# Root-mean-square norm: the last halving of the squares moves from VectorE to TensorE, and the last output tile is scaled on GpSimd

## The chip, the cores and the metric

The kernel runs on one core of a Trainium2 chip. The metric is the device time in microseconds of one execution; lower is better. One execution was profiled; the span of its profile runs from the first to the last instruction.

## The reference

Two layers (DEPTH = 2) work on x, 256 tokens by 1024 channels, in float32. Each begins with a root-mean-square norm, then a wide projection, three mixing branches (a recurrent one, a stick-breaking attention, a differential attention), gates, and an output projection that is added to x. A second norm feeds a convolutional feed-forward network, also added to x. A last norm gives the output. What matters here is the norm, five times in all:

```python
def rms_norm(x, g):
    xf = x.astype(jnp.float32)
    y = xf * lax.rsqrt(jnp.mean(xf * xf, axis=-1, keepdims=True) + EPS)
    return (y * g.astype(jnp.float32)).astype(x.dtype)

for l in range(DEPTH):
    h = rms_norm(x, norm_mix_g[l])          # norm 0 and norm 2
    ...
    x = x + merged @ w_out[l]
    x = x + conv_ffn(rms_norm(x, norm_ffn_g[l]), ...)   # norm 1 and norm 3
return rms_norm(x, norm_final_g)            # the last norm
```

## The kernel before

The activations lie transposed: 1024 channels are 8 tiles (KT) of 128 partitions, the 256 tokens (T) are the free dimension. The weights come as a stream of slabs of 128x1024 float32 through a ring of four buffers. SyncE issues the loads. ScalarE rounds a slab to a high half (`hi`), VectorE subtracts to get the low half (`lo`, line 1305), and TensorE multiplies with three products for each 128x128 block (`split_mm`: high by high, high by low, low by high). The activations are split in the same way into `hh` and `hl`. Each product is a matmul of 128x128 by 128x256.

Each engine has its own instruction list and runs it in order. For the mixing part the order is written out by hand: `STEPS` for TensorE, `ACT_STEPS` for ScalarE, `DVE_STEPS` for VectorE. A step `D n` is a slab (TensorE multiplies it; the other two split slab n+3), `E n` empties its result, and the steps of the branches lie between. The feed-forward part comes after these lists, as a loop over turns. Semaphores tie the lists together.

The norm is not applied to x before the product. The raw x, times the gain, is split and multiplied at once, and the factor of a token (`rs`) is applied when a result is emptied. So TensorE can start on slabs before the factor is known. To get the factor:

- ScalarE squares the 8 tiles of x into `XSQ`.
- VectorE adds them in halves in `add_squares`: 4 tiles on 4 (128x1024 elements), 2 on 2 (128x512), 1 on 1 (128x256, line 1321). `own.mark` and `own.wait` order one addition behind the other on VectorE; `DVE_OWN["layer"]` is the number of such marks in a layer. The last addition raises `squared`.
- TensorE in `norm(n)` multiplies an all-ones 128x128 block with the one tile that is left. This sums over the partitions and puts the sum of each token in every partition of bank 4, columns 0 to 255. For even n (the mixing part) two more matmuls, with the squares as the stationary operand and one column of ones as the moving one, put the sums as columns 256 and 257, token by partition: the value projections need the factor in this form. Odd n (the feed-forward part) doesn't use it.
- ScalarE in its own `norm(n, b, w)` takes a logarithm and an exponential of w columns (line 915 is the helper through which its activations go), and raises `rms_inv`. VectorE multiplies what it empties by `rs`.

TensorE runs norm 0 and norm 2 behind slab D2, norm 1 and norm 3 behind the first two slabs of the feed-forward part. Line 468 is the helper `mm`, so nearly all matmuls carry this line.

The last norm is written out at the end: ScalarE and VectorE scale the eight tiles of x by the gain into `HF`, TensorE sums squares, ScalarE makes `rs`, then VectorE multiplies four pairs of tiles of `HF` by `rs` (128x512 elements each, line 1801). SyncE stores each pair behind its `y_ready` (line 435), 256 KB each. GpSimd has little to do: clearing a block of constants once in a layer (line 450), and a few transfers; its last is the load of parameters that is issued when the last convolution is done.

Of the kernel before, what the change touches and what calls it, by code (L numbers as in the profile page):

```python
# [34 lines left out]
ALU = mybir.AluOpType  # L35
# [144 lines left out]


ACT_OWN = {"turn": 0, "layer": 16}
DVE_OWN = {"turn": 8, "layer": 125}


class Own:
# [16 lines left out]
def hybrid_blocks(nc, x_t, w_in, mix_in, ffn_in, fin_in, cf_in, cb_in, y_out):  # L203
    DEPTH = w_in.shape[0] // SLABS
    with ExitStack() as ctx:
# [144 lines left out]
        partner_in = [sem("query_partners_in"), sem("key_partners_in")]  # L350
        gates_ready = sem("gates_ready")
        merged_b, merged = sem("merged_b"), sem("merged")
        y_ready, y_stored = sem("y_ready"), sem("y_stored")
        last_scaled, square_pairs = sem("last_scaled"), sem("square_pairs")
        up_scaled, low_out = sem("up_scaled"), sem("low_out")
        rated_x, rated_h, rated_l = sem("rated_x"), sem("rated_h"), sem("rated_l")
# [57 lines left out]
        @block.sync  # L414
        def _(sp):

            sp.dma_start(raw[:, 0, HALF[0]], w_in[0, :, HALF[0]]).then_inc(first_in, 16)
            sp.dma_start(pm[:, 0:UPS], mix_in[0, :, 0:UPS]).then_inc(mix_in_s, 16)
            sp.dma_start(raw[:, 0, HALF[1]], w_in[0, :, HALF[1]]).then_inc(raw_in[0], 16)
            sp.dma_start(x[:, X_PART[2], :], x_t[:, X_PART[2], :]).then_inc(x_in[2], 16)  # L420
            for s in (1, 2):
                sp.dma_start(raw[:, s], w_in[s]).then_inc(raw_in[s], 16)
            sp.dma_start(cf[:, :], cf_in).then_inc(const_in, 16)
            sp.dma_start(raw[:, 3], w_in[3]).then_inc(raw_in[3], 16)
            sp.dma_start(cb[:, :], cb_in).then_inc(const_in, 16)
            sp.dma_start(pm[:, UPS:], mix_in[0, :, UPS:]).then_inc(ups_in_s, 16)
            with sp.Fori(1, DEPTH * SLABS // RING + 1) as i:
                for s in range(RING):

                    sp.wait_ge(hi_done, RING * i + (s - RING + 1))  # L430
                    sp.wait_ge(lo_done, RING * i + (s - RING + 1))
                    sp.dma_start(raw[:, s], w_in[RING * i + s]).then_inc(raw_in[s], 16)
            for b in range(4):
                sp.wait_ge(y_ready, b + 1)
                sp.dma_start(y_out[:, 2 * b:2 * b + 2, :], HF[:, 2 * b:2 * b + 2, :]).then_inc(y_stored, 16)
            sp.wait_ge(y_stored, 64)
            sp.wait_ge(ups_in_s, 16 * DEPTH + 16)
            sp.wait_ge(mix_in_s, 16 * DEPTH + 16)
            sp.wait_ge(ffn_in_s, 16 * DEPTH + 16)
            for s in range(RING):  # L440
                sp.wait_ge(raw_in[s], 16 * (DEPTH * SLABS // RING + 1))

        @block.gpsimd
        def _(pool):
# [3 lines left out]
            for l in range(DEPTH):  # L448
                pool.wait_ge(act_["kk"], n_of("kk", l, 1))
                pool.memset(BX, 0.0).then_inc(ones_set, 1)  # L450
                pool.wait_ge(ones_set, 3 * l + 1)
                for a in range(2):
                    pool.memset(BX[:, BASE * a:BASE * a + 33 * (BASE - 1) + 1:33], 1.0).then_inc(ones_set, 1)
                pool.wait_ge(act_["o"], n_of("o", l, BT))
                for i in range(2):
                    pool.wait_ge(*n_out(l, (OUT_CQ, OUT_CK)[i]))
                    for m in range(2):
                        for b in range(2):
                            to, of = HD * m + 8 * b, HD * m + 8 * (1 - b)
                            pool.dma_start(PARTNER[i][to:to + 8], (qc, kc)[i][of:of + 8, :, :])\  # L460
                                .then_inc(partner_in[i], 16)
                pool.wait_ge(conv_done, l * 2 * FT + 2 * FT)
                pool.dma_start(pf[:, :], ffn_in[l + 1]).then_inc(ffn_in_s, 16)

        @block.tensor
        def _(pe):
# [100 lines left out]

            def norm(n):

                pe.wait_ge(squared, n + 1)  # L570
                last = mm(bank[4][:, 0:T], cst("ones"), XSQ[:, 0, :], True, n % 2 == 1)
                if n % 2 == 0:

                    for tok in range(2):
                        last = mm(bank[4][:, T + tok:T + tok + 1], XSQ[:, 0, tok * P:(tok + 1) * P],
                                  cst("ones")[:, 0:1], False, True)
                last.then_inc(pe_["norm"], 1)

            def step(l, s):
# [326 lines left out]
        def _(act):  # L906
# [307 lines left out]
            for l in range(DEPTH):  # L1214
# [5 lines left out]
                act.wait_ge(ffn_in_s, 16 * l + 16)  # L1220
                ahead(l, FFN0)
                ahead(l, FFN0 + 1)
                norm(2 * l + 1, 4, T)
                act.preload_act_table(ACT.Silu)
                for t in range(2):
                    for which in range(2):
# [52 lines left out]
        def _(dve):  # L1279
# [35 lines left out]
            def add_squares(n):  # L1315
                dve.wait_ge(square_done, 4 * n + 4)
                own.mark(tt(XSQ[:, 0:4, :], XSQ[:, 0:4, :], XSQ[:, 4:8, :], ALU.add))
                own.wait()
                own.mark(tt(XSQ[:, 0:2, :], XSQ[:, 0:2, :], XSQ[:, 2:4, :], ALU.add))
                own.wait()  # L1320
                tt(XSQ[:, 0, :], XSQ[:, 0, :], XSQ[:, 1, :], ALU.add).then_inc(squared, 1)

            def lo_merged(l, cp):
                pair = slice(2 * cp, 2 * cp + 2)
# [467 lines left out]
            for c in (6, 7):  # L1792
                dve.tensor_scalar(HF[:, c, :], x[:, c, :], fin[:, c:c + 1], None, ALU.mult).then_inc(last_scaled, 1)
            dve.wait_ge(rms_inv, 2 * DEPTH + 1)
            for b in range(4):
                pair = HF[:, 2 * b:2 * b + 2, :]
                if b < 3:
                    dve.wait_ge(scaled, 2 * b + 2)
                else:
                    dve.wait_ge(last_scaled, 2)  # L1800
                tt(pair, pair, rep(rs[:, 0:T], 2), ALU.mult).then_inc(y_ready, 1)
        return nc

# [131 lines left out]
```

## Time and profile before

| | us |
|---|---|
| time, median of 3 runs | 1030.92 |
| the three runs | 1030.43, 1030.92, 1035.43 |
| time of the profiled execution | 1030.43 |
| its span | 1028.6 |
| TensorE busy in the span | 1009.4 (98%) |
| VectorE busy | 817.9 (80%) |
| ScalarE busy | 623.8 (61%) |
| GpSimd busy | 11.9 (1%) |

In the profile, PE is TensorE's matmuls and PEld its weight loads, DVE is VectorE, ACT ScalarE, POOL GpSimd, SPq the issues on SyncE's queue. A float32 matmul that isn't split by hand appears as two records. Matmuls are pipelined: the length of a record holds its way through the array too, so the cost of one is read from the distance between two starts, not from its length. The time of the profiled execution is 1.83 us above its span.

### The profile page before, as it was taken

Reading aid. Unit: us, or ns where it says so; the run is one execution under the profiler, and the core shown is the slowest. Engines: PE = TensorE matmul, PEld = TensorE weight load, DVE = VectorE, ACT = ScalarE, POOL = GpSimd, SP = SyncE. Lnnn points to the kernel's source line nnn. Section 1 sums busy time; section 2 is a strip of 40 time slices with the busy share of each in tenths; the row PEclk is TensorE's granted clock in tenths of the full one; section 3 lists DMA queues with packets and bytes.
Section 4 is the critical chain, followed back from the end, with each engine's and each line's share of the span. In section 5 each row is a group of like instructions: output and inputs, shape, how many; then the busy total and the mean of one; then the engine's idle time right before and its main releaser. Section 6 shows DMA issues by size and latency. Waiting matters only on the chain.

```text
span 1028.6 us, 22704 instructions
## 1 busy us (share of the span) xinstructions
PE 1009.4 (98%) x8522; PEld 945.2 (92%) x8522; DVE 817.9 (80%) x1363; ACT 623.8 (61%) x975; POOL 11.9 (1%) x30
## 2 busy tenths in 40 slices
PE   9999999999999999999999999999999999999997
PEld 8998888889999999999999989789999999999996
DVE  6799763797787898878778986649978879887876
ACT  7963433666656666666689543246666666666765
POOL 0000000100000000000000000010000000000000
PEclk9999999999999999999999999999999999999999
DMA  8442432326445565555534424233445536555553
GB/s 296 169 165 104 145 104 82 125 94 203 145 166 180 167 205 192 181 196 180 196 124 162 168 83 164 84 113 103 145 144 179 190 144 205 199 186 190 184 185 127
DMA packets 46283, 163.94 MB, mean 159 GB/s; under 512 B 5904, under 2 KB 6080, under 8 KB 46192
## 3 DMA queue, kind: packets, MB, share of 16 engines
q1 hardware_dynamic: 44640, 160.19, 45.4%
q10 hardware_dynamic: 864, 1.63, 0.5%
q8 instruction: 68, 1.11, 0.4%
q0 software_dynamic: 688, 0.81, 0.3%
q14 instruction: 23, 0.19, 0.1%
HBM read 161.04 MB, written 1.05 MB: 158 GB/s over the span
## 4 chain that ended last, share of the span: by engine, by line
PE 88%; DVE 8%; ACT 2%; issue 1%; DMA 1%; SPq 0%; DVEq 0%; ACTq 0%
PE psum L468 87%; DVE sb_lo L1305 2%; ACT sb_rw L915 1%; DVE sb_inv L1545 1%; DVE sb_inv L1513 1%; DVE sb_inv L1516 1%; PE psum L785 1%; DMA sb_raw<-w_stream 1%; DVE sb_yf L1569 0%; DVE sb_rw L1588 0%; ACT sb_hh L915 0%; DVE sb_inv L1490 0%; ACT sb_inv L915 0%; PE psum L823 0%; DVE sb_inv L1560 0%
## 5 line engine op out<-in xcount | busy, mean ns | idle before, releaser
L1305 DVE TENSOR_TENSOR sb_lo<-sb_raw,sb_hi 128x1024 fp32r<-128x1024 f32 x296 | 358.1, 1219 | 68.2 <-ACT sb_hi L915 67.8
L915 ACT ACTIVATE sb_hi<-sb_raw 128x1024 fp32r<-128x1024 f32 (+1 forms) x298 | 310.8, 1051 | 147.8 <-PE psum L468 139.4
L468 PE MATMUL psum<-sb_hh,sb_hi 128*128 128x256 f32 x1184 | 344.1, 291 | 2.0 <-DVE sb_hl L1312 1.3
L468 PE MATMUL psum<-sb_o,sb_hi 128*128 128x256 f32 (+1 forms) x1728 | 339.6, 308 | 1.3 <-DVE sb_o L1326 1.3
L468 PE MATMUL psum<-sb_hl,sb_hi 128*128 128x256 f32 x1184 | 336.0, 284 | 0.0
L468 PE MATMUL psum<-sb_hh,sb_lo 128*128 128x256 f32 x1184 | 335.8, 284 | 0.0
L468 PEld LDWEIGHTS psum<-sb_o,sb_hi 128*128 128x128 f32 x1728 | 278.6, 191 | 14.1 <-DVE sb_o L1326 1.7
L468 PE MATMUL psum<-sb_o,sb_lo 128*128 128x256 f32 x1056 | 243.7, 283 | 0.0
L468 PEld LDWEIGHTS psum<-sb_hh,sb_hi 128*128 128x128 f32 x1184 | 227.8, 192 | 14.8 <-issue 11.2
L468 PEld LDWEIGHTS psum<-sb_hl,sb_hi 128*128 128x128 f32 x1184 | 228.1, 193 | 0.7 <-issue 0.5
L468 PEld LDWEIGHTS psum<-sb_hh,sb_lo 128*128 128x128 f32 x1184 | 227.9, 192 | 0.0
L468 PEld LDWEIGHTS psum<-sb_o,sb_lo 128*128 128x128 f32 x1056 | 181.4, 191 | 3.7
L915 ACT ACTIVATE sb_rw<-psum 128x256 f32<-128x256 f32 (+4 forms) x96 | 38.4, 409 | 93.2 <-PE psum L468 85.5
L915 ACT ACTIVATE sb_rw<-sb_rw,sb_pf 128x256 f32<-128x256 f32 x88 | 52.3, 598 | 27.9 <-DVE sb_rw L1653 19.6
L1677 DVE SCALAR_TENSOR_TENSOR sb_rw<-sb_rw,sb_pf 128x254 f32<-128x254 f32 x88 | 42.5, 483 | 8.4 <-DVE sb_rw L1675 0.9
L915 ACT ACTIVATE sb_inv<-psum 128x256 f32<-128x256 f32 (+2 forms) x68 | 27.9, 445 | 32.1 <-PE psum L468 15.8
L915 ACT ACTIVATE sb_rw<-sb_rw 128x256 f32<-128x256 f32 (+3 forms) x70 | 41.9, 608 | 5.3 <-DVE sb_rw L1588 4.1
L915 ACT ACTIVATE sb_o<-sb_rw 128x256 fp32r<-128x256 f32 (+2 forms) x58 | 29.7, 511 | 24.4 <-DVE sb_rw L1684 19.9
L1675 DVE SCALAR_TENSOR_TENSOR sb_rw<-sb_rw,sb_pf 128x255 f32<-128x255 f32 x88 | 42.0, 477 | 2.2 <-ACT sb_rw L915 2.2
L1658 DVE TENSOR_TENSOR sb_rw<-sb_rw,psum 128x256 f32<-128x256 f32 x48 | 20.0, 416 | 10.7 <-ACT sb_rw L915 10.7
L468 PE MATMUL psum<-sb_rw 64*64 64x64 f32 (+3 forms) x298 | 27.2, 313 | 1.2 <-DVE sb_rw L1705 1.2
L468 PE MATMUL psum<-sb_inv 64*64 64x64 f32 x768 | 23.0, 221 | 3.7 <-ACT sb_inv L915 2.6
(180 smaller groups left out, 932.6 us busy)
## 6 DMA issues: line engine op xcount, KB each, us to landing
sb_raw<-w_stream SPq DMA_DIRECT2D x299, 512.0 KB, 3.4
sb_pm<-mix_par ACTq DMA_DIRECT2D x2, 512.5 KB, 3.5
y_t<-sb_rw SPq DMA_DIRECT2D x4, 256.0 KB, 2.4
sb_cf<-const_f SPq DMA_DIRECT2D x1, 550.0 KB, 9.0
sb_pm<-mix_par SPq DMA_DIRECT2D x1, 512.5 KB, 9.6
sb_raw<-w_stream SPq DMA_DIRECT2D x2, 256.0 KB, 4.7
sb_x<-x_t ACTq DMA_DIRECT2D x2, 256.0 KB, 4.6
sb_x<-x_t SPq DMA_DIRECT2D x1, 512.0 KB, 6.5
```

The costliest lines, as they stand in the source:

```text
L468: return pe.matmul(out, lhsT, rhs, start=start, stop=stop, skip_group_check=True)
L785: last = pe.transpose(bank[3 + 2 * j + b][:, cols], TAKE[j][:, hp * 384 + n * P:hp * 384 + (n + 1) * P], cst("ident"))
L915: return act.activation(out, in_, func, scale=scale, bias=bias, **kw)
L1305: tt(lo[:, s, :], raw[:, s, :], hi[:, s, :].bitcast(F32), ALU.subtract).then_inc(lo_done, 1)
L1513: own.mark(tt(tmp, ba[:, r, :, n:].unsqueeze(1).broadcast_to([P, n, 2, m]), bx[:, 0:n, :, r].unsqueeze(3).broadcast_to([P, n, 2, m]), ALU. ...
L1516: ins = tt(bx[:, 0:n, :, n:], bx[:, 0:n, :, n:], tmp, ALU.subtract)
L1545: ins = tt((ABT if what == "ab" else KBT)[:, j, 2 * b:2 * b + 2, :], bank[b0 + b][:, :].rearrange("p (i n) -> p i n", i=2), rep(both, 2), ...
L1658: tt(UM[:, k, :], UM[:, k, :], bank[k][:, 0:T], ALU.add).then_inc(up_scaled, 1)
L1675: own.mark(stt(CV[:, k, 1:T], UM[:, k, 0:T - 1], tap(col, 1), CV[:, k, 1:T], ALU.mult, ALU.add))
L1677: stt(CV[:, k, 2:T], UM[:, k, 0:T - 2], tap(col, 0), CV[:, k, 2:T], ALU.mult, ALU.add)\
```

## The change

Four things change.

1. `add_squares` on VectorE leaves out its third addition; `squared` is raised by the second. The count of marks in a layer falls from 125 to 123.
2. `norm(n)` on TensorE sums two tiles of squares instead of one: two matmuls with the all-ones block, and four with one column, two for each half of the tokens. It does so for every n: odd n no longer leaves out the columns.
3. The feed-forward norm on ScalarE takes 258 columns, as the other does.
4. At the end the last pair of tiles is multiplied by `rs` on GpSimd, not on VectorE, with a semaphore `y_last` of its own.

```diff
-DVE_OWN = {"turn": 8, "layer": 125}
+DVE_OWN = {"turn": 8, "layer": 123}
...
             for b in range(4):
-                sp.wait_ge(y_ready, b + 1)
+                if b < 3:
+                    sp.wait_ge(y_ready, b + 1)
+                else:
+                    sp.wait_ge(y_last, 1)
                 sp.dma_start(y_out[:, 2 * b:2 * b + 2, :], HF[:, 2 * b:2 * b + 2, :]).then_inc(y_stored, 16)
...
+            pool.wait_ge(last_scaled, 2)
+            pool.wait_ge(rms_inv, 2 * DEPTH + 1)
+            pool.tensor_tensor(HF[:, 6:8, :], HF[:, 6:8, :], rs[:, 0:T].unsqueeze(1).broadcast_to([P, 2, T]), ALU.mult)\
+                .then_inc(y_last, 1)
...
                 pe.wait_ge(squared, n + 1)
-                last = mm(bank[4][:, 0:T], cst("ones"), XSQ[:, 0, :], True, n % 2 == 1)
-                if n % 2 == 0:
-
+                for c in range(2):
+                    mm(bank[4][:, 0:T], cst("ones"), XSQ[:, c, :], c == 0, False)
+                for c in range(2):
                     for tok in range(2):
-                        last = mm(bank[4][:, T + tok:T + tok + 1], XSQ[:, 0, tok * P:(tok + 1) * P],
-                                  cst("ones")[:, 0:1], False, True)
+                        last = mm(bank[4][:, T + tok:T + tok + 1], XSQ[:, c, tok * P:(tok + 1) * P],
+                                  cst("ones")[:, 0:1], False, c == 1)
                 last.then_inc(pe_["norm"], 1)
...
-                norm(2 * l + 1, 4, T)
+                norm(2 * l + 1)
...
                 own.mark(tt(XSQ[:, 0:4, :], XSQ[:, 0:4, :], XSQ[:, 4:8, :], ALU.add))
                 own.wait()
-                own.mark(tt(XSQ[:, 0:2, :], XSQ[:, 0:2, :], XSQ[:, 2:4, :], ALU.add))
-                own.wait()
-                tt(XSQ[:, 0, :], XSQ[:, 0, :], XSQ[:, 1, :], ALU.add).then_inc(squared, 1)
+                tt(XSQ[:, 0:2, :], XSQ[:, 0:2, :], XSQ[:, 2:4, :], ALU.add).then_inc(squared, 1)
...
-            for b in range(4):
+            for b in range(3):
                 pair = HF[:, 2 * b:2 * b + 2, :]
-                if b < 3:
-                    dve.wait_ge(scaled, 2 * b + 2)
-                else:
-                    dve.wait_ge(last_scaled, 2)
+                dve.wait_ge(scaled, 2 * b + 2)
                 tt(pair, pair, rep(rs[:, 0:T], 2), ALU.mult).then_inc(y_ready, 1)
```

## Rows read from the trace of the kernel before

**Rows 1.** Chain that ended last, in order of time: start us, length us, what.

```profile
8.78 63.60 PE psum L468 x498
...
73.55 1.23 DVE sb_rw L1479
...
343.36 169.02 PE psum L468 x1230
...
520.99 56.39 PE psum L468 x456
...
848.36 173.77 PE psum L468 x1260
```

**Rows 2.** Busy time in one stretch: PE, PEld, DVE, ACT, POOL, clock, DMA share, GB/s.

```profile
331.00:512.00 181.00, 180.97 (x1331) 172.53 (x1330) 151.67 (x251) 118.58 (x182) 0.57 (x1) 1.00 0.55 187
```

**Rows 3.** Timeline, TensorE at norm 0: start us, length us, what.

```profile
18.78 0.28 PE L468 MATMUL psum<-sb_hh,sb_lo 128*128 128x256 f32 x1
18.90 0.59 PE L468 MATMUL psum<-sb_rw,sb_cf 128*128 128x256 f32 x2
19.33 0.50 PE L468 MATMUL psum<-sb_cf,sb_rw 128*128 128x1 f32 x4
19.69 0.36 PE L468 MATMUL psum<-sb_small,sb_cf 128*128 128x2 f32 x2
19.91 0.36 PE L468 MATMUL psum<-sb_hh,sb_hi 128*128 128x256 f32 x1
20.11 0.28 PE L468 MATMUL psum<-sb_hl,sb_hi 128*128 128x256 f32 x1
```

**Rows 4.** Timeline, TensorE at norm 1.

```profile
331.12 0.28 PE L468 MATMUL psum<-sb_hh,sb_lo 128*128 128x256 f32 x1
331.24 0.59 PE L468 MATMUL psum<-sb_rw,sb_cf 128*128 128x256 f32 x2
331.48 0.47 PE L468 MATMUL psum<-sb_hh,sb_hi 128*128 128x256 f32 x1
331.78 0.28 PE L468 MATMUL psum<-sb_hl,sb_hi 128*128 128x256 f32 x1
```

**Rows 5.** Timeline around norm 0 and norm 2, with VectorE's idle time before.

```profile
16.42 0.42 DVE L1321 TENSOR_TENSOR sb_rw<-sb_rw 128x256 f32<-128x256 f32 x1
...
21.84 0.42 DVE L1357 TENSOR_TENSOR sb_qb<-psum,sb_rs 128x256 f32<-128x256 f32 x1 [2.03 <-ACT sb_rs L915]
...
523.12 0.42 DVE L1321 TENSOR_TENSOR sb_rw<-sb_rw 128x256 f32<-128x256 f32 x1
...
523.96 0.59 PE L468 MATMUL psum<-sb_rw,sb_cf 128*128 128x256 f32 x2
```

**Rows 6.** Timeline, first step of the mixing part behind norm 0 that joins the engines.

```profile
25.87 0.76 PEld L468 LDWEIGHTS psum<-sb_rw,sb_pm 64*128 64x128 f32 x8 [0.16 <-issue]
```

**Rows 7.** Timeline, VectorE where the chain leaves TensorE.

```profile
72.41 1.23 DVE L1477 TENSOR_TENSOR sb_rw<-sb_rw 128x1024 f32<-128x1024 f32 x1 [0.38 <-PE psum L468]
```

**Rows 8.** Timeline of the end, VectorE and SyncE's queue; last, issue to landing (L435).

```profile
1023.11 2.50 DVE L1801 TENSOR_TENSOR sb_rw<-sb_rw,sb_rs 128x512 f32<-128x512 f32 x4 [1.22 <-ACT sb_rs L915]
1023.83 2.14 SPq L435 DMA_DIRECT2D y_t<-sb_rw  x4
...
DMA to landing us min/median/max: 2.2/2.4/2.6
```

**Rows 9.** Busy time in stretches of the end, columns as in rows 2.

```profile
1024.50:1025.00 0.50, 0.00 (x0) 0.00 (x0) 0.50 (x2) 0.00 (x0) 0.00 (x0) 1.00 0.60 229
1025.00:1025.50 0.50, 0.00 (x0) 0.00 (x0) 0.50 (x2) 0.00 (x0) 0.00 (x0) 1.00 1.05 385
...
1027.00:1027.50 0.50, 0.00 (x0) 0.00 (x0) 0.00 (x0) 0.00 (x0) 0.00 (x0) 0.82 0.97 361
1027.50:1028.00 0.50, 0.00 (x0) 0.00 (x0) 0.00 (x0) 0.00 (x0) 0.00 (x0) 0.50 0.04 8
```

**Rows 10.** GpSimd's clearing of constants, by line: count, ns min/median/max, starts.

```profile
L450 POOL MEMSET sb_inv<- x2: 526/528/529, 50.7 to 555.6; 128x512 f32 x2
```

More of the change, by code:

```diff
@@ L352, in hybrid_blocks @@
         merged_b, merged = sem("merged_b"), sem("merged")
-        y_ready, y_stored = sem("y_ready"), sem("y_stored")
+        y_ready, y_last, y_stored = sem("y_ready"), sem("y_last"), sem("y_stored")
         last_scaled, square_pairs = sem("last_scaled"), sem("square_pairs")
```

## The prediction

> **What bounds the kernel now.** I read the chain of work that ended last first, since the change moves work between engines and only the engine on that chain turns work into time. It lies on TensorE in long unbroken pieces: 8.78 to 72.4, 343.4 to 512.4, 521.0 to 577.4 and 848.4 to 1022.1 us [rows 1]. A small part, as that at 73.6, goes over VectorE. The four norms that the change touches start at 18.90, 331.24, 523.96 and (norm 1 one layer on, 523.96 - 18.90 = 505.0 us later) 836.2 us on TensorE. The first and third lie inside pieces of the chain that are shown. For the other two I looked at the busy time by stretches: in 331 to 512 us TensorE is busy 180.97 of 181.00 us [rows 2], so it has nothing to wait for, and whatever it gets in addition pushes the rest back. The reader should see that TensorE is full there while VectorE is at 84% (151.67 of 181).
>
> Then I read the timeline of TensorE at norm 0 and norm 1 [rows 3, 4] for the price of its instructions, that of VectorE around them [rows 5] for what its third addition costs and whether anyone waits for it, and the end of the kernel [rows 8, 9] for the store of the output.
>
> **The change part by part.**
>
> *The third addition on VectorE.* It takes 0.42 us, four times [rows 5]. Who waits for it? At norm 0 it ends at 16.84, and TensorE comes to the norm at 18.90, 2.1 us later, from running matmuls. At norm 2 it ends at 523.54 and TensorE comes at 523.96; this 0.42 us is the smallest margin. So TensorE never waits for `squared`. What stands behind the addition on VectorE's list? Splits of slabs, and then the first use of `rs`, before which VectorE is idle for 2.03 us at norm 0 [rows 5]. The 0.42 us only lengthens that wait. Gain: 0.
>
> *The matmuls on TensorE.* A split product starts every 0.12 us. At norm 0 the all-ones matmul starts at 18.90 and the next one at 19.33: 0.43 us. Two one-column matmuls (four records) run from 19.33 to 19.69: 0.18 each. The matmul of the lambda values and the change back to the stream take from 19.69 to 20.11, against 0.12 for one start of the stream: 0.30 [rows 3]. At norm 1 there is one all-ones matmul: from 331.24 to 331.78, less the 0.12 of the product between, 0.42 us with the change back [rows 4].
>
> - Even norms (0 and 2) get one all-ones matmul (0.43) and two one-column ones (0.36): +0.79 us each.
> - Odd norms (1 and 3) had 0.42. Now two all-ones matmuls (0.86), three one-column ones (0.54) and a fourth with the change back (0.30): 1.70, so +1.28 us each.
> - Sum: 2 x 0.79 + 2 x 1.28 = 4.14 us, all on the chain.
>
> Is some of it hidden? Behind norm 0, TensorE's first step that depends on the other engines' use of `rs` starts with 0.16 us of idle time in front [rows 6]. If that is a wait for ScalarE, and not a change between forms, TensorE's delay takes it up. So an even norm costs 0.63 to 0.79. Further on, VectorE's work at 72.41 is released by TensorE, after 0.38 us of idle time [rows 7]. There the chain leaves TensorE, and the delay goes with it. The other engines get `rs` later by less than or the same as TensorE's own next slabs, so no new wait of TensorE on them arises. The bounds of this part are 2 x 0.63 + 2 x 1.28 = 3.8 and, if each of the twelve added one-column matmuls (2 + 4 + 2 + 4) costs the 0.30 of the one with the change back and not 0.18, 12 x 0.12 = 1.4 more, 5.6.
>
> *The wider columns on ScalarE.* Two more columns in two instructions a layer: 256 or 258 make no difference that these rows could show. 0.
>
> *The marks and semaphores.* One wait less per addition on VectorE, at no one's cost. SyncE's queue waits for `y_last` in front of the last store; nothing stands behind it but the final waits. GpSimd waits for `last_scaled` and `rms_inv` with nothing behind it either; its last transfer was issued before. 0.
>
> *The last pair on GpSimd.* Before, VectorE multiplies four pairs from 1023.11 to 1025.61, about 0.62 us apart, and SyncE issues the four stores from 1023.83; the last issue, of 0.33 us, starts at 1025.64 [rows 8]. A hasty reader would take 0.62 us off. But the transfers are what ends last: from 1024.7 to 1027.5 they run at 360 to 390 GB/s without a gap, and stop [rows 9]. At 375 GB/s a store of 256 KB takes 0.70 us and four take 2.8 us, more than the 0.62 us at which VectorE delivers. The first store's data moves 0.85 us after its issue. For the last one that would be 1026.5, while the three in front of it are done at 1024.7 + 3 x 0.70 = 1026.8. So the last store is queued, with 0.3 us in hand, and to issue it earlier brings nothing. If it were worth anything it is at most 0.3 us, since its issue can't come before that of the third pair is over. Its gain is 0.
>
> What does the multiplication take on GpSimd? The trace has none. The nearest row is its clearing of 128x512 elements: 0.528 us, with one stream, the writing [rows 10]. Lower bound 0.53; with two reads and the write one after another 1.58. I take two streams' worth, 1.06 us (the reads can't be free, the write runs behind them). It starts with VectorE's first pair at 1023.11 and so ends at 1024.2 (1024.7 by the upper bound), before VectorE's third pair at 1025.0. It is not late by any of these.
>
> GpSimd has two tensors to read at the same time as VectorE's three multiplications, each of which reads two tensors of SBUF as well. If they run side by side, the cost is 0. If they exclude each other, it is not: see the rivals. The rows of before show no such pair of instructions. The Trainium skill ("SBUF — State Buffer", section "SBUF: two separate sides") speaks against this part of the change: a VectorE instruction with two SBUF inputs and a GpSimd instruction that reads SBUF lock a shared pair of ports, and whoever comes second is blocked for the whole of the other's instruction. By it the sum would be that of rival B. For the duration the skill ("GPSIMD Engine Reference", section "3.1 Elementwise — side-by-side cycle accounting") gives 4,497 ns for 2048 float32 elements; a quarter of it is 1.12 us (an estimate from that page), near what I took, and the sum would be the same.
>
> *Sum.* 4.14 on TensorE, 0 elsewhere. The profiled execution has 1028.6 us of span and 1.83 around it, 1030.43: that gives 1034.6. It is the fastest of the three runs, and the median is 0.49 above it: from the median it is 1035.1. I say 1034.8, in the middle.
>
> **The rivals.**
>
> *B: the two engines exclude each other at the end, and the kernel is slower by half a per cent.* If VectorE is first, its pair 0 is on time, GpSimd takes 1.06, pair 1 is ready at 1025.4 instead of 1024.4 and its data starts at about 1026.25; three stores of 0.70 follow: 1028.35 against 1027.5, +0.85. If GpSimd is first, all pairs are 1.06 late: +1.06 (1.58 with the upper bound). Both engines wait for the same semaphore, so either can be. For it: they do start together. Against it: nothing in the rows. It decides as soon as the lock costs the second store more than 0. Total 4.14 + 0.85 to 1.6: 1035.5 to 1036.6, about 1035.8, and 5.1 us is 0.5% of 1030.43.
>
> *C: GpSimd is much slower than its clearing suggests.* The last store has 0.3 us in hand, so GpSimd's result costs time from 1025.9 on, which is 2.8 us after its start; that is five times its 0.528 us. Each us beyond costs one. With twice that, 5.6 us: +2.8, 1037.6. A first use of a routine could do this. The Trainium skill ("GPSIMD Engine Reference", section "2.1 Instruction dispatch") gives approximately 6 us for the first call of a freshly loaded kernel; by it the multiplication would end at 1030.2, and the total would be near 1039 (an estimate from that page); no run here shows such a load.
>
> *D: part of TensorE's addition is hidden in the mixing part.* If VectorE or ScalarE, not TensorE, sets the time at the joint at 25.9 or at 72.4 us, the 0.79 us of an even norm vanishes, twice: 4.14 - 1.58 = 2.56, 1033.2. For it: from 73.6 on the chain is on VectorE, with TensorE still fed. Against: VectorE was idle 0.38 us for TensorE's result at 72.41 [rows 7], so at least that part less the 0.38 must come through even if the chain were another.
>
> *E: no slower at all.* VectorE's relief would have to be on the path, 4 x 0.42 = 1.7 us, and TensorE's 4.14 us would have to fall into idle time. It would need TensorE to be waiting for `squared`; the smallest margin is 0.42 us the other way, and TensorE's idle time in 331 to 512 us is 0.03 us [rows 2].
>
> **How the numbers follow.** The forecast (A) 0.53, B 0.27, C 0.06, D 0.10, E 0.04. The range of 8 in 10 reaches from D's upper half to B's upper part: 1033.0 to 1036.6; C and E and the rest of D are left out, and A's own is 1034.2 to 1036.0 by the bounds of the matmuls. Less than 0.5% (5.2 us) is about what a measurement here can't tell from no change. A, at 0.4%, lies within it, as D and E do; B lies on the line, half of it beyond; C is beyond; and a small part of A is, if the matmuls cost more (0.06). So slower 0.26, faster 0.01, the same 0.73.
>
> **What would show it right or wrong.** In the changed kernel's timeline, norm 0 should hold two all-ones matmuls 0.43 us apart and four one-column ones 0.18 apart, and TensorE should have no new idle time. The first use of `rs` on VectorE should show more idle time than 2.03 us less what ScalarE hides. The starts behind each norm should move by 0.8, 2.1, 2.9 and 4.1 us in total against those of before. A shift that is there behind norm 0 but gone at 72.4 is D. At the end, the durations of VectorE's multiplications (0.62 us apart before) and the start of GpSimd's tell A from B: blocked instructions would show as longer or later. The transfers should again be without a gap for 2.8 us and start as long after `rs` as before. The prediction is wrong if the shift behind a norm is not that of the matmuls, if the transfers start later or have a gap, or if a wait of TensorE appears that was not there.

## The result, and the profile after

| | before | changed |
|---|---|---|
| median, us | 1031.85 (17 runs) | 1038.35 (17 runs) |
| lowest and highest, us | 1030.23, 1035.43 | 1035.03, 1039.20 |
| profiled execution, us (span) | 1030.43 (1028.6) | 1038.57 (1036.8) |

The changed kernel takes 1.0058 of the time of before, 95% interval 1.0048 to 1.0067: slower by 0.6%. The forecast was 1034.8 us, range 1033.0 to 1036.6. The measured time lies 1.75 us above the range. Executions of the changed kernel spread over 4 us, and the profiled one lies in the upper group. One execution of a later kernel (shift_between, 1390.8 us at a mean granted clock of 0.655) was in another state of the chip than all the others and is left out of its ratio and its count.

I read the new profile in the order in which the forecast says the shift should grow. First the matmuls of norm 0 and norm 1, on the timeline of TensorE (start us, length us, what). They answer to [rows 3] and [rows 4].

```profile
18.65 0.28 PE L475 MATMUL psum<-sb_hh,sb_lo 128*128 128x256 f32 x1
18.77 1.02 PE L475 MATMUL psum<-sb_rw,sb_cf 128*128 128x256 f32 x4
19.63 0.95 PE L475 MATMUL psum<-sb_cf,sb_rw 128*128 128x1 f32 x8
20.44 0.36 PE L475 MATMUL psum<-sb_small,sb_cf 128*128 128x2 f32 x2
...
20.87 0.28 PE L475 MATMUL psum<-sb_hl,sb_hi 128*128 128x256 f32 x1
...
333.43 0.28 PE L475 MATMUL psum<-sb_hh,sb_lo 128*128 128x256 f32 x1
333.55 1.02 PE L475 MATMUL psum<-sb_rw,sb_cf 128*128 128x256 f32 x4
334.41 0.95 PE L475 MATMUL psum<-sb_cf,sb_rw 128*128 128x1 f32 x8
...
335.42 0.28 PE L475 MATMUL psum<-sb_hl,sb_hi 128*128 128x256 f32 x1
```

Norm 0 takes 20.87 - 18.65 = 2.22 us from the last product in front to the second behind, against 1.33 before: +0.89. Norm 1 takes 1.99 against 0.66: +1.33. The two all-ones matmuls are 0.43 apart, as forecast; a one-column matmul takes 0.20 (0.81 for four), not 0.18.

But norm 1 starts at 333.55, which is 2.31 us later than before, where 0.8 was expected. Something between norm 0 and norm 1 has cost 1.6 us. The busy times by stretches have a column for the granted clock (the third from the end), and there it is:

```profile
151.00:157.00 6.00, 5.20 (x184) 4.52 (x185) 5.25 (x12) 2.58 (x5) 0.00 (x0) 1.00 0.51 178
159.80:163.20 3.40, 3.40 (x10) 2.72 (x10) 0.33 (x2) 0.00 (x0) 0.00 (x0) 0.50 0.00 0
668.40:671.80 3.40, 3.40 (x11) 2.81 (x11) 0.54 (x2) 0.00 (x0) 0.00 (x0) 0.50 0.00 0
```

TensorE runs at half clock (1.2 instead of 2.4 GHz) for 3.4 us, once in each layer, right behind the stretch where it has only 64-wide matmuls of the recurrent branch to do (151 to 159 us, and the same in layer 2). I call this a fall of the clock. The timeline shows the dense slab behind it stretched: its products start 0.43 us apart (160.31, 160.74) and, from 163.27 on, 0.23 us again (163.27, 163.50).

In the profiled execution of before, the same slab starts at 159.07 and the next one at 162.74; here it is 159.77 and 165.01. That is 5.24 against 3.67 us: 1.57 us for one fall of the clock. Up to the fall the shift is 0.70 us, near the 0.89 - 0.13 = 0.76 that the matmuls of norm 0 alone would give. Of before, this is the stretch by the same view:

```profile
150.00:159.00 9.00, 7.88 (x218) 6.92 (x216) 7.57 (x17) 2.58 (x5) 0.00 (x0) 1.00 0.35 120
159.00:162.40 3.40, 3.40 (x20) 2.88 (x20) 0.44 (x2) 0.00 (x0) 0.00 (x0) 1.00 0.00 0
```

The share of busy time in the stretch doesn't tell the two apart. In equal windows that end where the slab or the half clock begins, TensorE is counted busy 7.58 of 8.70 us in both layers of before (150.3 to 159.0, 655.3 to 664.0), with no fall behind; 7.78 and 7.47 of 8.70 us in the changed kernel (151.0 to 159.7, 659.7 to 668.4), with a fall behind each.

The other norms start at 527.34 and 842.37, and the last logarithm is at 1029.30. The whole way:

| start of | before | changed | shift | grown by |
|---|---|---|---|---|
| norm 0 | 18.90 | 18.77 | -0.13 | |
| norm 1 | 331.24 | 333.55 | 2.31 | 2.44 |
| norm 2 | 523.96 | 527.34 | 3.38 | 1.07 |
| norm 3 | 836.24 | 842.37 | 6.13 | 2.75 |
| last `rs` (ScalarE's logarithm) | 1022.16 | 1029.30 | 7.14 | 1.01 |
| end of span | 1028.64 | 1036.76 | 8.13 | 0.99 |

From norm 0 to the last `rs` it is 7.27 us; less two falls of 1.57 us that leaves 4.13.

Each odd norm inserts 1.33 but shows only 1.0 to 1.1 further on. The difference goes 12 us behind it. In the kernel before TensorE waits there for VectorE's `lo` of a slab, which ends at 343.31:

```profile
343.36 0.19 PEld L468 LDWEIGHTS psum<-sb_hh,sb_hi 128*128 128x128 f32 x1 [0.23 <-DVE sb_lo L1305]
```

From the product at 343.06 to the second one behind it (343.58) it is 0.52 us, where two starts of the stream are 0.24. In the changed kernel `lo` is ready at 346.70, TensorE comes later, and the same step takes 0.27 (346.70 to 346.97). So 0.25 us of the insertion falls into a wait that was there before; behind norm 3, at 848.36, it is about as much.

Between norm 2 and norm 3 it is the other way: 2.75 less 1.57 is 1.18, and the insertion is only 0.89. In the middle of the 64 products of the last step of the sparse stretch of layer 2, TensorE stands still, and nothing that the profile shows released it ("issue"). The second line is from a later kernel, split_norm, which has no fall:

```profile
665.56 0.97 PE L475 MATMUL psum<-sb_inv 64*64 64x64 f32 x14 [0.74 <-issue]
...
663.02 1.36 PE L468 MATMUL psum<-sb_inv 64*64 64x64 f32 x17 [0.54 <-issue]
```

In layer 2 of the profiled execution of before TensorE has no such pause inside these products, only one of 0.69 us behind them, for VectorE's result. What the profile does show is a transfer on the DMA queue of instructions: 16 KB land at 664.19 in the changed kernel and at 661.65 in split_norm, and TensorE goes on 1.4 us later in both. So the pause looks like a wait for the engine's own code; more on it below.

Then the end, the timeline of VectorE, GpSimd and SyncE's queue, and VectorE's line by itself (count, ns min/median/max). It answers to [rows 8].

```profile
1030.26 2.97 DVE L1804 TENSOR_TENSOR sb_rw<-sb_rw,sb_rs 128x512 f32<-128x512 f32 x3 [1.22 <-ACT sb_rs L923]
1030.38 1.69 POOL L469 TENSOR_TENSOR sb_rw<-sb_rw,sb_rs 128x512 f32<-128x512 f32 x1 [10.45 <-ACT sb_rs L923]
1030.98 3.10 SPq L438 DMA_DIRECT2D y_t<-sb_rw  x4
...
L1804 DVE TENSOR_TENSOR sb_rw<-sb_rw,sb_rs x3: 679/693/1755, 1030.3 to 1032.5; 128x512 f32<-128x512 f32 x3
```

Three multiplications on VectorE take 2.97 us, more than four took before (2.50). Two have their old length, and the second, which lies beside GpSimd's, takes 1.755 us, 1.07 more. GpSimd's starts at 1030.38 and its end, 1032.07, is 1.1 us after the end of VectorE's first (about 1030.95): it got through only when that one was out of the way, and then VectorE's second had to wait. The stores have a hole for it. These two lines cut 1030 to 1037 us in 40 slices; the first is the busy share of the DMA engines in tenths, the second the GB/s:

```profile
DMA  0000000000599930000099999999999900000000
GB/s 0 0 0 0 0 0 0 0 0 0 222 374 386 386 129 0 0 0 0 12 374 386 374 386 386 351 410 386 328 363 386 339 12 0 0 0 0 0 0 0
```

Four slices of 0.175 us are empty behind the first store, where before there was no gap [rows 9]. From the start of the last `rs` to the end of the span it is 7.46 us, against 6.48 before: the end costs 0.98 us.

### The profile page after: what moved, and what is told of

Its sections match the earlier page's. It is cut to its first block, busy times and chain, and to the rows that moved or that the text cites. A ratio compares the mean times of both kernels' runs of the same rounds, so it can differ in the third digit from the quotient of the medians.

```text
span 1036.8 us, 22767 instructions
## 1 busy us (share of the span) xinstructions
PE 1014.6 (98%) x8554; PEld 949.2 (92%) x8554; DVE 817.7 (79%) x1358; ACT 624.2 (60%) x975; POOL 13.7 (1%) x31
## 3 DMA queue, kind: packets, MB, share of 16 engines
HBM read 161.04 MB, written 1.05 MB: 156 GB/s over the span
## 4 chain that ended last, share of the span: by engine, by line
PE 88%; DVE 7%; ACT 2%; issue 1%; DMA 1%; SPq 0%; DVEq 0%; ACTq 0%
PE psum L475 87%; DVE sb_lo L1313 2%; ACT sb_rw L923 1%; DVE sb_inv L1551 1%; DVE sb_inv L1519 1%; DMA sb_x<-x_t 1%; DVE sb_inv L1522 1%; PE psum L793 1%; ACT sb_hh L923 0%; DVE sb_rw L1594 0%; DVE sb_inv L1496 0%; ACT sb_inv L923 0%; PE psum L831 0%; DVE sb_inv L1566 0%; DVE sb_rw L1485 0%
```

## The experiments

The three terms (matmuls, clock, end) were taken apart by leaving each out. Times are medians; "before" of the same chip session was 1031.22, 1031.20, 1031.94 and 1031.01 in the four sessions. For the clock I also count executions whose mean granted clock was 0.997 or more. A fall to half for 3.4 us takes 0.0017 off that mean, but so does one between 8 and 16 us, which 11 of the 16 profiled executions have, and half clock behind the last matmul, which all have. So the count is a rough one: of the 16 profiled executions 8 have no fall behind a sparse stretch, and 3 of these 8 (shift_between, warm_before, split_before) have a mean under 0.997. All 8 with a fall have one under 0.997. The record lists the clock of 19 executions of the changed kernel and the time of 17.

| kernel | runs | median | lowest | ratio, 95% interval | clock 0.997 or more |
|---|---|---|---|---|---|
| before, all sessions | 91 | | 1029.97 | | 37 of 91 |
| changed | 17 | 1038.35 | 1035.03 | 1.0048 to 1.0067 | 4 of 19 |
| tail_only | 11 | 1031.88 | 1031.38 | 0.9999 to 1.0017 | 5 of 11 |
| norm_only | 5 | 1037.19 | 1035.39 | 1.0033 to 1.0061 | 1 of 5 |
| even_only | 11 | 1033.82 | 1031.74 | 1.0012 to 1.0030 | 5 of 11 |
| odd_only | 10 | 1034.09 | 1033.04 | 1.0015 to 1.0034 | 4 of 10 |
| warm_before | 11 | 1032.83 | 1032.47 | 1.0003 to 1.0031 | 8 of 11 |
| warm_norm | 5 | 1037.22 | 1036.77 | 1.0031 to 1.0068 | 5 of 5 |
| pe_load | 6 | 1038.13 | 1037.00 | 1.0041 to 1.0074 | 0 of 6 |
| tail_after_dve | 12 | 1032.18 | 1030.74 | 0.9992 to 1.0020 | 6 of 12 |
| shift_early | 12 | 1033.56 | 1032.65 | 1.0006 to 1.0034 | 5 of 12 |
| shift_between | 12 | 1035.20 | 1032.77 | 1.0014 to 1.0040 | 1 of 11 |
| split_before | 9 | 1029.31 | 1028.75 | 0.9961 to 0.9987 | 5 of 9 |
| split_after | 12 | 1035.23 | 1033.95 | 1.0019 to 1.0039 | 6 of 12 |
| shift_far | 6 | 1034.20 | 1033.94 | 1.0010 to 1.0043 | 3 of 6 |
| split_norm | 5 | 1034.53 | 1033.25 | 1.0021 to 1.0048 | 3 of 5 |

**The end alone (tail_only).** The kernel before with part 4 of the change and nothing else.

> Only the last pair's multiplication is moved to GpSimd; the norms are as before. Theory L (the two engines exclude each other): the second of VectorE's three multiplications takes about 1.75 us instead of 0.69, the store's transfers show a gap of about 1 us, and the kernel is 1.0 to 1.1 us slower (0.10%). Theory S (GpSimd is only slow, no exclusion): VectorE's three stay at 0.69 us each, and the time changes by 0 to 0.3 us. By theory K (the granted clock falls because of the norms' changed matmuls), executions with the clock at half speed in the recurrent part are as rare here as in the kernel before.

Its timeline, GpSimd and VectorE:

```profile
1023.17 2.96 DVE L1805 TENSOR_TENSOR sb_rw<-sb_rw,sb_rs 128x512 f32<-128x512 f32 x3 [1.22 <-ACT sb_rs L922]
...
1023.29 1.69 POOL L469 TENSOR_TENSOR sb_rw<-sb_rw,sb_rs 128x512 f32<-128x512 f32 x1 [10.46 <-ACT sb_rs L922]
```

2.96 and 1.69 us again. The ratio's interval includes 1, so the time by itself doesn't decide; its profiled span, 1029.7 without a fall in the stretches, is 1.1 us above the 1028.6 of before, and the lowest execution is 1.4 us above before's lowest. From the last `rs` to the end it is 7.46 us, as in the changed kernel, against 6.48 before. Theory L holds by the durations.

**The end, one after the other (tail_after_dve).** GpSimd also waits for VectorE's third pair.

```diff
             pool.wait_ge(rms_inv, 2 * DEPTH + 1)
+            pool.wait_ge(y_ready, 3)
```

> The last pair is multiplied on GpSimd, but only after VectorE's three are done (the norms as before). Theory L (the engines exclude each other): all of VectorE's take 0.69 us again, GpSimd's alone takes 1.0 to 1.15 us against 1.69 beside VectorE, the last store is issued at about 0.6 us later than before and with 0.3 us in hand costs +0.3 us: 0.7 us better than with both at once. Theory S (GpSimd is only slow): GpSimd's takes 1.7 us here too, and the kernel is +0.9 us.

VectorE's line and GpSimd's:

```profile
L1806 DVE TENSOR_TENSOR sb_rw<-sb_rw,sb_rs x3: 684/685/693, 1025.5 to 1026.7; 128x512 f32<-128x512 f32 x3
...
L470 POOL TENSOR_TENSOR sb_rw<-sb_rw,sb_rs x1: 1257/1257/1257, 1027.6 to 1027.6; 128x512 f32<-128x512 f32 x1
```

Alone, GpSimd's multiplication takes 1.257 us, a little above the upper of what I expected (1.15), and VectorE's are all at 0.69. Both engines were lengthened by running together: VectorE's by 1.07 us, GpSimd's by 0.43. So they exclude each other; that is shown. From the last `rs` to the end it is 6.93 us: 0.53 less than with both at once (0.7 expected) and 0.45 more than before (0.3 expected). The lowest execution (1030.74) is 0.6 us below tail_only's (1031.38). The medians don't tell it: tail_after_dve is 0.98 us above its before and tail_only 0.66.

**The norms alone (norm_only)** and **each kind of norm alone (even_only, odd_only).** The changed kernel with the old end; then with the new form for even or for odd n only, in TensorE's `norm` and VectorE's `add_squares` alike.

> The norms are changed, the end is as before. The matmuls alone give +4.1 us. Theory K (the changed norms make the granted clock fall to half behind norm 0 and norm 2, 1.6 us each): +4.1 in executions without a fall, +5.7 with one, +7.3 with both, and most have both. Theory M (the clock fell by chance, whatever the kernel): falls as often as in the kernel before.

> Only norms 0 and 2 are changed. By the matmuls +1.6 us. Theory K: both falls of the clock remain, since both lie behind an even norm, so +4.7 us. Theory M: +1.6 us as a rule.

> Only norms 1 and 3 are changed. By the matmuls +2.6 us. Theory K, if it is the change of an even norm just ahead that counts: no fall, +2.6 us. If any shift of TensorE counts, then only the second fall (behind norm 2, after norm 1's shift): +4.1 us.

norm_only is 6.0 us above its before, even_only 2.6, odd_only 2.9. The matmuls insert 2 x 0.89 = 1.8 us, and 2 x 1.33 = 2.7 of which 2 x 1.05 = 2.1 comes through. So even_only and odd_only each have 0.8 us more than their matmuls, and norm_only 2.1 us more than the 3.9 of its own. That both together bring more than the sum of the two parts (6.0 against 5.5 us) isn't shown: the interval of norm_only's five runs is 2.9 us wide. The profiled executions of even_only and odd_only have one fall each, at 666.8 and 664.6 us, and norm_only's has a double one, 6.8 us long, in layer 2 and none in layer 1. So theory K as it stands, a fall behind each even norm, fits neither even_only nor norm_only. The expectation for odd_only by theory K (+2.6 or +4.1) is met at its lower end; even_only's +4.7 is missed.

**TensorE's load without VectorE's relief (pe_load).**

```diff
                 pe.wait_ge(squared, n + 1)
+                mm(bank[4][:, 0:T], cst("ones"), XSQ[:, 0, :], True, n % 2 == 1)
+                for col in range(T + 4, T + 4 + (2 if n % 2 == 0 else 4)):
+                    mm(bank[4][:, col:col + 1], XSQ[:, 0, (col % 2) * P:(col % 2 + 1) * P], cst("ones")[:, 0:1], False,
+                       True)
                 last = mm(bank[4][:, 0:T], cst("ones"), XSQ[:, 0, :], True, n % 2 == 1)
```

> VectorE keeps its third addition; TensorE runs as many matmuls in each norm as in the changed kernel (the added ones repeat the sum or write columns that nobody reads). If TensorE's matmuls alone are the cost and VectorE's relief is worth nothing: the same as the changed norms alone, +3.8 to +4.1 us in executions without a fall of the clock, 1036 to 1037.5 in the median. If VectorE's relief was worth its 4 x 0.42 us: 1.7 us slower than the changed norms alone.

1038.13, 0.9 us above norm_only, midway between the two expectations, and with overlapping intervals (1.0041 to 1.0074, 1.0033 to 1.0061). None of its six executions has a mean clock of 0.997 or more, and the profiled one has a double fall in layer 2, as norm_only's. So TensorE's matmuls alone bring both the time and the falls. The medians don't settle what VectorE's relief is worth, but the two timelines do. From the start of norm 0 to the last `rs` pe_load takes 1030.99 - 20.29 = 1010.70 us and norm_only 1029.21 - 18.50 = 1010.71, with the same fall. In this pair the relief is worth nothing; the 1.8 us between the two spans lie ahead of norm 0.

That last point holds for all: norm 0 starts between 18.18 and 20.29 us in the 16 profiled executions, at 19.44 or later in the five with 6.8 us at half clock between 8 and 16 us, and at 18.18 to 19.45 in the others. So a part of the spread of the times, up to 2 us, arises ahead of norm 0 and has nothing to do with the sparse stretches.

**Matmuls of no use in the gaps (warm_before, warm_norm).** Before the waits of the products in the sparse stretch:

```diff
                 elif kind == "dxy":
+                    if c == 2:
+                        for _ in range(2 if s[2] == LEVELS[-1] else 1):
+                            mm(bank[3][:, 0:T], cst("ones"), cst("cos"), True, True)
                     pe.wait_ge(dve_["m1"], n_of("m1", l, ORD[("m1", c, s[2])] + 1))
```

> The kernel before, with four full-width matmuls (constants, 0.43 us each, result unused) put in each layer into the gaps of TensorE in the stretch of 64-wide matmuls at 150 to 159 us and 655 to 664 us. Theory K2 (the granted clock falls because that stretch keeps TensorE too little occupied): no fall behind it any more; executions at 1030.5 to 1031.2, no second group at 1032 to 1033; about 0.1 to 0.5 us is lost where the four don't fit the gaps, so the median is 0 to 0.7 us lower than before. Theory M (chance that has nothing to do with that stretch): falls as often, and the time 0.2 to 0.8 us higher.

> The changed norms without the changed end, with the same four matmuls in the gaps. Theory K2: no falls, 1034.5 to 1035.2, that is +4.1 by the matmuls of the norms and little else; 2 us under the run with the changed norms alone (1037.2). Theory M: about 1037.

The clock part came out, the time part didn't. Neither profiled execution has a fall behind the stretches, all five executions of warm_norm have a clock of 0.997 or more where norm_only had one of five, and the spread shrinks: 1036.77 to 1037.78. But the four matmuls cost 1.0 us in layer 1 (norm 0 to norm 1: 313.34 against 312.34 us) and 1.3 in layer 2 (313.56 against 312.28). They are 4 x 0.43 = 1.7 us of work, and TensorE's idle times in the stretch are only 0.13, 0.25 and 0.69 us; some 0.1 us at each change of form would account for the rest. So the gain was paid back. The difference between warm_norm and warm_before is the norms' matmuls with the falls taken away from both: 1037.22 - 1032.83 = 4.4 us. That this equals 2 x 0.89 + 2 x 1.33 = 4.44 is luck. By the starts of the norms the difference grows by 0.88, 1.07, 1.55 and 1.01 us: the odd norms show 0.6 us less than they insert, and 0.7 us more are lost in the sparse stretch of layer 2, where TensorE has the pause named above (0.59 us in warm_norm, none in warm_before).

**Useful work in the gaps (split_before, split_after, split_norm).** Slab 36 has twelve products in four groups. Group 0 now goes ahead of the 32-wide `dxy` step, group 1 ahead of the 64-wide one, and the other two stay.

```diff
+            def dense_group(l, n, g):
+                s, i = n % RING, DENSE[n][1]
+                if g == 0:
+                    pe.wait_ge(lo_done, l * SLABS + n + 1)
+                tt, k2 = divmod(g, 2)
+                k, cols, tok = 2 * i + k2, slice(k2 * BW, (k2 + 1) * BW), slice(tt * P, (tt + 1) * P)
+                last = split_mm(bank[BANK[OUT_OF[n][tt]]][:, :], (hh[:, k, tok], hl[:, k, tok]),
+                                (hi[:, s, cols], lo[:, s, cols]), k == 0, k == KT - 1)
+                if g == 3:
+                    last.then_inc(slab_done, 1)
...
+                elif kind == "D" and s[1] == 36:
+                    dense_group(l, 36, 2)
+                    dense_group(l, 36, 3)
...
                 elif kind == "dxy":
+                    if c == 2 and s[2] > LEVELS[0]:
+                        dense_group(l, 36, LEVELS.index(s[2]) - 1)
```

> The kernel before, with a slab that TensorE has to do anyway (the 36th, twelve products of 128x128 by 128x512 in four groups of 0.70 us) no longer wholly behind the sparse stretch: one group goes into its gap of 0.46 us and one into that of 0.90 us. By theory K2 (the clock falls because of the low occupation of that stretch) falls get rare, and the gaps are filled with work that counts: 0.9 to 1.2 us less in each of the two layers, 1028.5 to 1029.0 without a fall, median 2.0 to 2.7 us under that of before. If the falls don't depend on that stretch: 1028.5 to 1029 in half of the executions and 1030 to 1031.5 in the others.

> The changed kernel with the same move of half a slab. By theory K2: no falls, and 1030.5 + 4.4 (matmuls of the norms as measured) + 1.1 (the end) - 2.1 = 1033.9; that is 4.4 us under the changed kernel's 1038.35. If falls stay: 1036 to 1037.

> The changed norms without the changed end, with half of the 36th slab in the gaps of the sparse stretch. The matmuls of the norms, without falls of the clock: 1029.3 + 2 x 0.89 + 2 x 1.33 = 1033.7 by the distances between starts in the changed kernel's timeline; 1033.4 if the forecast's 4.14 was right. The difference to the same kernel with the changed end (1035.2) should be that of the end alone, 1.0 us.

split_before is the fastest kernel of this study: 1029.31 us, 0.9974 of before (0.9961 to 0.9987). TensorE's stretch in it is nearly full, and the clock stays at full behind it:

```profile
150.00:159.00 9.00, 8.81 (x212) 7.03 (x211) 7.17 (x15) 2.58 (x5) 0.00 (x0) 1.00 0.38 120
```

8.81 us busy of 9, against 7.88. The work that moved into the gaps saves 0.66 us in layer 1 and 0.61 in layer 2 (norm to norm, 311.68 and 311.67 us, no fall in either execution), less than the 0.9 to 1.2 expected. The median is 2.6 us below its before (expected 2.0 to 2.7); the other 1.3 us would be falls that are gone, which is argued from the medians. The same move takes 3.1 us off the changed kernel (1038.35 to 1035.23; expected 4.4), which would fit that the changed kernel had more falls to lose. The mean clocks still vary (6 of 12 at 0.997 or more), so that not every fall is shown to be gone. split_norm was expected at 1033.7 and came out at 1034.53 with its lowest at 1033.25; 0.7 us of the difference to split_before are again lost in the stretch of layer 2, with the pause of 0.54 us. split_after less split_norm is 0.7 us for the end (expected 1.0); from the last `rs` to the end it is 7.46 and 6.48 us, 0.98.

None of the five profiled executions with the gaps filled has a fall behind a stretch (ten stretches). Of the eleven others, nine of 22 stretches have one.

**Why are falls more frequent? (shift_early, shift_between, shift_far).** The kernel before with 5 or 8 more all-ones matmuls in one norm of layer 1:

```diff
                 pe.wait_ge(squared, n + 1)
+                for _ in range({0: 5, 1: 0}.get(n, 0)):
+                    mm(bank[4][:, 0:T], cst("ones"), XSQ[:, 0, :], True, n % 2 == 1)
```

> The kernel before, with five more all-ones matmuls (the same sum again) in norm 0 alone: 5 x 0.43 = 2.15 us, ahead of both sparse stretches, so that both come later by the same amount and their distance stays 505.0 us. Theory P (the falls of the clock behind the two stretches come together or apart, depending on the distance of the two stretches, which the changed norms alter by 2.2 us): as in the kernel before, in about half of the executions there is no fall, and the lowest group lies at 1032.6. Theory Q (any added work on TensorE ahead of a stretch makes the fall more frequent): hardly an execution without one, median 1035 or more.

> The same five matmuls in norm 1 alone, between the two sparse stretches: 2.15 us, and the distance of the stretches grows to 507.2 us, as in the changed kernel. Theory P: a fall in nearly every execution, at one of the two stretches, median near 1034.5. Theory Q: the fall at the first stretch as often as before (nothing ahead of it is changed), so executions without any fall are a third or more.

> The kernel before, with eight more all-ones matmuls in norm 1 alone: 8 x 0.43 = 3.4 us, so the distance of the two sparse stretches grows from 505.0 to 508.4 us. Every stretch at half clock in the records so far is 3.4 us long or 6.8; if it is the distance of the sparse stretches that decides how the falls of the two layers go together (theory P), a distance larger by that very length acts as the old one: 4 to 6 of 10 executions without a fall, at 1033.9 to 1034.6. Theory Q (more work on TensorE ahead of a stretch, more falls): at least as few without a fall as with 2.15 us at the same place (3 of 11), median 1036 to 1037.

The same 2.15 us of work gives 1033.56 at norm 0, ahead of both sparse stretches, and 1035.20 at norm 1, between them. Within 1.2 us of its lowest execution lie 7 of 12 of shift_early, 2 of 11 of shift_between, and 4 of 6 of shift_far, which has more added work than either at the same place as shift_between and is 1.0 us faster than it. That speaks against the added work as such (theory Q). The counts go as theory P says, with the distance between the two layers' sparse stretches. They are small, though, the intervals of the three ratios overlap, and the profiled execution of shift_between has no fall at all. I take P as supported, not as shown.

A rival was not tested: the pause of TensorE inside the 64 products of the stretch's last step. Its place depends on how many matmuls have been added to the norms ahead of it. In layer 2 it stands behind 62 of the 64 products with five added (odd_only, shift_early, shift_between), 60 with six (even_only), 56 with eight (shift_far) and 50 with eleven (changed, norm_only, pe_load): two products earlier for each added matmul. It ends 1.3 to 1.5 us after 16 KB have landed on the DMA queue of instructions, in all of these. In before the 64 products are done by that time, and the pause costs nothing. In layer 2 changed, norm_only, even_only, odd_only and pe_load have pauses of 0.16 to 0.81 us, and each has a fall. The six others with unfilled gaps have none (three), 0.11 us (two) or 0.43 us (shift_far), and no fall. In layer 1 it doesn't divide them: six have a pause of 0.2 us or more, and three of these have a fall; shift_far has a fall without it. So whether the pause makes the fall more frequent stays open.

## Why the prediction was wrong

*What bounds the kernel.* Right for the even norms: at the slab behind the sparse stretch 0.83 of the 0.89 us of norm 0 are still there (norm 0 starts 0.13 us earlier than before, the slab 0.70 later), so rival D is out. TensorE did not wait for `squared`. Wrong in a part for the odd norms. "Busy 180.97 of 181.00 us, so it has nothing to wait for" took the length of records for work: a record reaches over the start of the next one and hides a short wait. TensorE waited about 0.25 us for VectorE's `lo` at 343.36 in that very stretch, and so much of each odd norm was hidden. The same reading was carried over to norm 3 without a row of its own.

*Matmuls, 4.14 us.* The size came out, 4.13 us by the table of shifts, but in part by luck. A one-column matmul costs 0.20 us, not 0.18, so the insertions are 0.89 and 1.33 (sum 4.44); 0.6 us of the two odd ones are hidden; and 0.3 us are lost in the sparse stretch of layer 2 that no matmul of a norm explains. In the pairs without falls, warm and split, that loss is 0.7 us.

*The last pair on GpSimd, 0 us.* Wrong, and rival B, given 0.27, is what happens. It costs 0.98 us in the profile. I had worked out 0.85 for the order "VectorE first", which was the actual one (VectorE, GpSimd, VectorE), and 1.06 for the other. The failed step is the overlap: the sum put the cost of the two engines reading side by side at 0, with no row that showed such a pair. There the Trainium skill ("SBUF — State Buffer", section "SBUF: two separate sides") had the rule that came true, a lock held for the whole of an instruction. The trace agrees: VectorE's blocked multiplication takes 1.755 us in the changed kernel, and all three take 0.69 in tail_after_dve. GpSimd's duration alone, 1.257 us, lay between my 1.06 and the upper bound 1.58, so rival C is out. That the store had 0.3 us in hand was about right: in tail_after_dve GpSimd's result comes 0.85 us later behind the last `rs` than VectorE's last pair did before, and the end is 0.45 us later.

*TensorE's clock.* This is the step that put the time outside the range, and the forecast doesn't have it: its sum has no term for the granted clock, which puts it at nothing without a reason. The sum, and all the rivals, took TensorE's speed as that of the one profiled execution of before, in which no fall lies in either stretch. With the matmuls (4.13) and the end (0.98) the sum would be 1030.43 + 5.1 = 1035.5, in the range, and the lowest executions (1035.03, 1035.48) are there. The profiled execution has two falls of 1.57 us each, and 4.13 + 0.99 + 3.14 - 0.13 = 8.13 us is the whole growth of its span (the 4.13 is what the falls leave over, so this is a balance and no separate proof). That the typical execution, at 1038.35, has one or two falls more than the fastest ones is argued from the times: 12 of the 17 lie at 1038.1 to 1039.2, by the profiled one with its two falls. The sign that I passed over was in the table of times: the three runs of before were 1030.43, 1030.92 and 1035.43, a spread that the profiled one, as the fastest, couldn't explain.

*What stays open.* Falls seem to exist in the kernel before too: 57 of its 108 executions lie more than 1.2 us above the lowest of their session, though its only profiled one has no fall. That the changed norms make them more frequent is in the counts: 5 of 30 executions with a clock of 0.997 or more for changed, norm_only and pe_load, against 37 of 91. That the sparse stretch has to do with them is supported by the fillers: 13 of 16 in the two warm kernels, and no fall in ten filled stretches. Why the changed norms make them more frequent is open: the distance between the layers' stretches and the pause of TensorE inside them are both possible.

## What to carry to other kernels

A change that shifts work on a full TensorE can cost more than the work: find the stretches where it has only small matmuls and gaps, ask for the granted clock behind them in more than one execution, and don't take the fastest execution as the kernel. Fill such gaps with work that has to be done anyway: here that gave 1.3 us by the work itself and 2.6 us in the median, while matmuls of no use didn't pay for themselves. Don't take a busy share near 1 on TensorE as a sign that it never waits; look at the distances between starts. Don't move the last of a few elementwise multiplications from VectorE to GpSimd to run beside the others: with two inputs each in SBUF they take turns, and here the transfers ended last anyway.

## What the runs showed of the hardware

- A VectorE multiplication of 128x512 float32 with two SBUF inputs, 0.69 us, took 1.755 us when GpSimd's like instruction was under way; GpSimd's took 1.69 us there and 1.257 us alone. VectorE went first and GpSimd second; both were released by ScalarE's `rs`, 0.12 us apart in their starts (1030.26, 1030.38).
- The granted clock fell from 2.4 to 1.2 GHz for 3.4 us (6.8 us in norm_only and pe_load) in nine of the 22 unfilled stretches profiled, and in none of ten filled ones. In the changed kernel that was right behind a stretch of 64-wide matmuls in which TensorE was counted busy 7.47 to 7.78 of 8.70 us and had no idle time over 0.81 us. In the same stretch of before, 7.58 of 8.70 us, the profiled execution had no fall. One fall cost 1.57 us.
- TensorE stood still for up to 0.81 us in a row of 64 like products, with no releaser in the profile, and went on 1.3 to 1.5 us after a 16 KB transfer on the DMA queue of instructions had landed. The place moved two products earlier for each float32 matmul added ahead of it (62, 60, 56, 50 of 64 with 5, 6, 8, 11 added).
- A float32 matmul of 128x128 by one column costs 0.20 us, nearly half of one by 256 columns (0.43 us). The change back to the split products costs some 0.1 us (0.20 against 0.12 us from start to start behind norm 1).
